# Down projection of the feed-forward stage: a different order of its weight units, and a split ahead of three additions to x

## The chip, the cores and the metric

The kernel runs on one core of one Trainium2 chip. The metric is the device time of one execution in microseconds (us); lower is better. Shown is the median of several runs, beside the time and the trace of one profiled execution.

## The reference, cut to what matters

Two blocks of two layers each work on x, 256 tokens by 1024 features in fp32. Every layer has two feed-forward stages (before and after a mixing stage), so there are eight of them:

```python
def swiglu(h, w1, w3, w2):
    return (jax.nn.silu(h @ w1) * (h @ w3)) @ w2

x = x + 0.5 * swiglu(rmsnorm(x, g), w1, w3, w2)      # w1, w3: 1024 x 2816, w2: 2816 x 1024
```

The change touches only the last product, with `w2`, called the down stage here.

## The kernel before, in words

**Splitting.** TensorE multiplies in fp32r. To keep fp32 accuracy every weight tile is split in two: ScalarE rounds it to `whi`, then VectorE computes the rest, `wlo = raw - whi`. Each product is three matmuls (hi by hi, hi by lo, lo by hi; lines 900, 902, 904 in `products`, lines 707, 708, 709 in `blocks`). The semaphores are `hi_done` (ScalarE's half is there), `w_ready` (VectorE's half too), `w_used` (TensorE is done with the unit). They are counters, so all engines go through the units in one common order.

**Units and buffers.** A unit is one slot of weights. Split units live in `split_w`, four slots (`HL`): ScalarE may split unit n only when TensorE is done with unit n - 4. Loads from HBM go to `raw`, three slots (`RAW`): the load of a unit may start only when VectorE has split the unit three loads earlier (SyncE waits in `load` on `w_ready`).

**The down stage.** 22 chunks of 128 hidden features are the depth. Ten of them are multiplied plainly: units ("plain", half, i), called P0, P1, P2 for the left 512 output columns and H0, H1, H2 for the right ones (here `half` 0 and 1). P0, P1, H0, H1 have 4 chunks (24 matmuls), P2 and H2 have 2 (12 matmuls). The other twelve are multiplied as 2 by 2 blocks with seven products instead of eight: U, 11, 21, T2, 22, T3, T4. Each of these has two units of 9 matmuls, a and b. The weights 11, 21, 22 are loaded to `raw`; U, T2, T3, T4 are sums of weight blocks. U, T2 and T4 are made in `early_sums` by accumulating DMAs that GpSimd issues (`down_sums`): T2 is U plus 22, T4 is T2 plus 21. T3 is made in `late_sums` by VectorE (`sum_added`), which adds the freshly loaded 22 to it. These sums take no slot of `raw`.

**The order.** The table `DOWN` gives the order of the units; ScalarE (`down_split` over the index), SyncE (`ffn_loads`) and the counts of all waits follow it. TensorE's and VectorE's code is written out in the same order by hand: in `ffn_tensor` behind `alone(0, 0, ...)`, in `ffn_vector` behind the loop over `i`. Before, it is

P0, Ua, Ub, 11a, 11b, 21a, 21b, P1, T2a, T2b, 22a, 22b, P2, T3a, T3b, T4a, T4b, H0, H1, H2.

VectorE also adds finished PSUM banks to x (`part_to_x`) between its splits. `used(i)` in front of one waits until TensorE is done with unit i, `split_before(i)` until VectorE's own split of unit i has ended. Banks: `EACH` is bank 0 (11, then T2, then T3 are accumulated there, with an addition to x taken between them; the semaphore `taken` tells TensorE that it may go on), `BOTH` is bank 1. Half way through H0, TensorE transposes the new x for the next stage; for that it waits until the last of these additions is done. `e.link` makes an engine wait for its own instruction.

Of the kernel before, what the change touches and what calls it, by code (L numbers as in the profile page):

```python
# [33 lines left out]
FG = FF // 256  # L34
# [8 lines left out]
SUPER, PAIRS = 2, 3  # L43
# [7 lines left out]
def each(kind, name):  # L51
    return tuple((kind, name, s) for s in range(SUPER))


DOWN = ((("plain", 0, 0),) + each("sum", "U") + each("quarter", "11") + each("quarter", "21") + (("plain", 0, 1),)
        + each("sum", "T2") + each("quarter", "22") + (("plain", 0, 2),) + each("sum", "T3") + each("sum", "T4")
        + tuple(("plain", 1, i) for i in range(3)))
# [149 lines left out]
def build(nc, a, known):  # L207
# [13 lines left out]
    with ctx:  # L221
# [460 lines left out]
        def _(eng):  # L682
# [112 lines left out]
            def ffn_tensor(u0, f, next_stage):  # L795
# [92 lines left out]
                def products(name):  # L888
# [3 lines left out]
                    for s in range(SUPER):  # L892
# [15 lines left out]
                def alone(half, i, start, stop):  # L908
                    blocks(u0 + 2 * FG + AT["plain", half, i], 0, 1 if half else 2, HT, ALONE[i], start, stop, True)
# [7 lines left out]
                products("21")  # L917
# [3 lines left out]
                products("T2")  # L921
                products("22")
                eng.wait_ge(ht_done, ffn_pairs(e, f, 10))
                alone(0, 2, False, (True, False))
                eng.wait_ge(taken, 2 * ffns(e, f) + 2)
# [915 lines left out]
        def _(eng):  # L1841
# [148 lines left out]
            def ffn_vector(u0, f, next_stage):  # L1990
# [117 lines left out]
                def splits(kind, name):  # L2108

                    for s in range(SUPER):  # L2110
                        i = at(kind, name, s)
                        added = [t for t, q in (("T2", "22"), ("T3", "22"), ("T4", "21")) if q == name and t in BY_VECTOR]
                        for t in added:
                            sum_added(u0 + 2 * FG + i, f, t, s)
                        down_split(i)

                splits("quarter", "11")
                splits("quarter", "21")
# [5 lines left out]
                splits("sum", "T2")  # L2124
                splits("quarter", "22")
                down_split(at("plain", 0, 2))
                used(at("sum", "T2"))
                split_before(at("plain", 0, 2))
                part_to_x(0, 1, EACH, minus_half).then_inc(taken, 1)
                splits("sum", "T3")  # L2130
                splits("sum", "T4")
                used(at("sum", "T3"))
                split_before(at("sum", "T4"))
                part_to_x(1, 0, EACH, rhalf)
                part_to_x(1, 1, EACH, minus_half)
                used(at("plain", 0, 2))
                part_to_x(0, 0, psum[:, 4, :], rhalf)
                down_split(at("plain", 1, 0))
                split_before(at("plain", 1, 0))
# [584 lines left out]
```

## Time and profile before

| what | value |
|---|---|
| median of 3 runs | 2255.55 us (2254.95 to 2256.36) |
| profiled execution, its time | 2255.33 us |
| profiled execution, its span | 2253.5 us |
| TensorE busy | 2226.4 us, 99% of the span |
| VectorE busy | 1711.6 us, 76% |
| ScalarE busy | 1305.8 us, 58% |
| DMA | 467.92 MB, mean 208 GB/s |
| granted TensorE clock | 1.0 of full speed on average |

Matmul records overlap (one starts every 0.23 us and is shown 0.39 us long), so idle time of TensorE is read best from the starts of its matmuls. A time such as t+8.16 below is counted from the first matmul of Ua in a stage. This matmul starts at 136.50 us in the first of the eight stages.

### The profile page before, as it was taken

The numbers are of one execution on the slowest core, as the hardware profiler recorded it, in microseconds if no ns is written. First come the engines' busy times: TensorE is split into PE (matmuls) and PEld (weight loads), VectorE is DVE, ScalarE is ACT, GpSimd is POOL, SyncE is SP. The second block draws the span as 40 slices with busy tenths as digits, with TensorE's granted clock in tenths as the row PEclk, the third lists the DMA queues.
The fourth block names the chain that finished last, engine by engine and source line by source line (L and its number), as shares of the span: only waits on it lengthen the run. The fifth ranks groups of instructions, "written<-read, shape, count | busy, mean of one in ns | idle before, by whom it ended". The sixth has DMA issues, their size and how long they took to land.

```text
span 2253.5 us, 28616 instructions
## 1 busy us (share of the span) xinstructions
PE 2226.4 (99%) x11542; PEld 1890.5 (84%) x11542; DVE 1711.6 (76%) x2067; ACT 1305.8 (58%) x1425; POOL 42.2 (2%) x52
## 2 busy tenths in 40 slices
PE   9999999999999999999999999999999999999999
PEld 8888888888887888887888888888888878888887
DVE  7876567868878566877887799768788777976876
ACT  7655445555655544655655676455565557754654
POOL 0000000000000000000000000000000000000000
PEclk9999999999999999999999999999999999999999
DMA  7876455767758455577576753547667575345756
GB/s 264 261 225 245 168 191 181 249 199 229 233 181 278 171 178 196 200 226 237 206 245 213 235 171 128 205 157 244 216 225 238 169 254 200 107 168 196 232 181 204
DMA packets 171859, 467.92 MB, mean 208 GB/s; under 512 B 18608, under 2 KB 22576, under 8 KB 171728
## 3 DMA queue, kind: packets, MB, share of 16 engines
q1 hardware_dynamic: 164672, 428.35, 53.8%
q0 software_dynamic: 6912, 37.75, 9.3%
q8 instruction: 91, 1.49, 0.3%
q14 instruction: 40, 0.33, 0.0%
q10 hardware_dynamic: 144, 0.00, 0.0%
HBM read 464.99 MB, written 1.05 MB: 207 GB/s over the span
## 4 chain that ended last, share of the span: by engine, by line
PE 87%; DVE 9%; DMA 2%; ACT 1%; issue 0%; SPq 0%; DVEq 0%; ACTq 0%
PE psum L771 25%; PE psum L772 13%; PE psum L707 12%; PE psum L709 12%; PE psum L708 12%; DVE split_w L1851 4%; PE psum L782 3%; PE psum L739 2%; PE psum L790 2%; DVE split_w L1858 1%; DVE x L2048 1%; DVE late_sums L1867 1%; PE psum L900 1%; PE psum L904 1%; PE psum L902 1%; DMA raw<-ffn_w_down_alone_dram 1%
## 5 line engine op out<-in xcount | busy, mean ns | idle before, releaser
L1851 DVE TENSOR_TENSOR split_w<-raw,split_w 128x2048 fp32r<-128x2048 f32 (+2 forms) x405 | 854.1, 2118 | 179.6 <-ACT split_w L1328 177.6
L771 PE MATMUL psum<-xt,split_w 128*128 128x512 f32 x2464 | 858.7, 393 | 0.5 <-DVE split_w L1851 0.5
L1328 ACT ACTIVATE split_w<-raw 128x2048 fp32r<-128x2048 f32 (+2 forms) x405 | 716.7, 1778 | 204.6 <-PE psum L709 95.2
L772 PE MATMUL psum<-xt,split_w 128*128 128x256 f32 x2464 | 688.1, 279 | 0.0
L771 PEld LDWEIGHTS psum<-xt,split_w 128*128 128x128 f32 x2464 | 461.3, 187 | 105.2 <-DVE split_w L1851 2.2
L772 PEld LDWEIGHTS psum<-xt,split_w 128*128 128x128 f32 x2464 | 464.9, 189 | 0.3
L707 PE MATMUL psum<-split_w,xt 128*128 128x512 f32 (+1 forms) x736 | 289.5, 393 | 0.0
L709 PE MATMUL psum<-split_w,xt 128*128 128x512 f32 (+1 forms) x736 | 283.7, 385 | 0.0
L708 PE MATMUL psum<-split_w,xt 128*128 128x512 f32 (+1 forms) x736 | 283.6, 385 | 0.0
L1997 DVE TENSOR_TENSOR gate_up<-psum,low 128x512 f32<-128x512 f32 x176 | 121.0, 688 | 144.1 <-ACT low L1403 144.1
L1403 ACT ACTIVATE low<-psum 128x512 f32<-128x512 f32 x176 | 104.1, 591 | 173.8 <-PE psum L772 158.3
L707 PEld LDWEIGHTS psum<-split_w,xt 128*128 128x128 f32 x736 | 138.3, 188 | 28.8 <-issue 3.0
L709 PEld LDWEIGHTS psum<-split_w,xt 128*128 128x128 f32 x736 | 138.2, 188 | 28.1
L708 PEld LDWEIGHTS psum<-split_w,xt 128*128 128x128 f32 x736 | 138.4, 188 | 25.6
L707 PE MATMUL psum<-split_w,ht_hi 128*128 128x512 f32 x316 | 125.3, 397 | 13.5 <-DVE split_w L1851 13.5
L1409 ACT ACTIVATE gate_up<-gate_up 128x512 f32<-128x512 f32 x88 | 55.7, 633 | 131.5 <-DVE gate_up L2004 131.5
L709 PE MATMUL psum<-split_w,ht_lo 128*128 128x512 f32 x316 | 123.3, 390 | 0.0
L708 PE MATMUL psum<-split_w,ht_hi 128*128 128x512 f32 x316 | 123.2, 390 | 0.0
L1349 ACT ACTIVATE xt<-psum,vecs 128x256 fp32r<-128x256 f32 x88 | 34.5, 476 | 108.1 <-PE psum L739 108.1
L782 PE MATMUL psum<-xt,split_w 128*128 128x512 f32 x352 | 86.1, 393 | 1.4 <-ACT split_w L1328 1.4
L2016 DVE TENSOR_TENSOR ht_lo<-hid,ht_hi 128x512 fp32r<-128x512 f32 x88 | 60.6, 688 | 35.3 <-ACT ht_hi L1414 35.3
L707 PEld LDWEIGHTS psum<-split_w,ht_hi 128*128 128x128 f32 x316 | 59.3, 188 | 31.8 <-issue 14.5
(305 smaller groups left out, 2839.2 us busy)
## 6 DMA issues: line engine op xcount, KB each, us to landing
raw<-w_in_dram SPq DMA_DIRECT2D x180, 512.0 KB, 4.4
raw<-t_gate_up_1b_dram SPq DMA_DIRECT2D x88, 512.0 KB, 4.7
raw<-t_gate_up_2a_dram SPq DMA_DIRECT2D x88, 512.0 KB, 4.7
raw<-t_gate_up_2b_dram SPq DMA_DIRECT2D x88, 512.0 KB, 4.7
raw<-t_gate_up_1a_dram SPq DMA_DIRECT2D x84, 512.0 KB, 4.8
early_sums<-ffn_w_down_quarters_dram POOLq DMA_DIRECT2D x24, 768.0 KB, 7.3
raw<-ffn_w_down_quarters_dram SPq DMA_DIRECT2D x48, 384.0 KB, 4.5
raw<-ffn_w_down_alone_dram SPq DMA_DIRECT2D x32, 512.0 KB, 7.1
```

The costliest lines, as they stand in the source:

```text
L707: nc.tensor.matmul(pair(p, m)[:, out], hi[:, c, t], whi[:, slot, w], start=first, stop=False)
L708: nc.tensor.matmul(pair(p, m)[:, out], hi[:, c, t], wlo[:, slot, w], start=False, stop=False)
L709: last = nc.tensor.matmul(pair(p, m)[:, out], lo[:, c, t], whi[:, slot, w], start=False, stop=final)
L771: nc.tensor.matmul(bank, whi[:, slot, w], xt[:, c, :, :], start=c == 0, stop=False)
L772: last = nc.tensor.matmul(bank[:, 0:T], wlo[:, slot, w], xt_hi[:, c, :], start=False, stop=c == DC - 1)
L782: nc.tensor.matmul(pair(p, j), whi[:, e.unit(u) % HL, first:first + P], xt[:, c, :, :], start=c == 0, stop=False)
L1328: nc.scalar.activation(whi[:, e.unit(u) % HL, 0:n], raw[:, r, 0:n], ACT.Copy).then_inc(hi_done, 1)
L1403: nc.scalar.activation(low[:, b % 2, :, :], psum[:, first:first + 2, T:2 * T], ACT.Copy).then_inc(low_done, 1)
L1409: nc.scalar.activation(gate_up[:, :, 0, :], gate_up[:, :, 0, :], ACT.Silu).then_inc(gate_done, 1)
L1851: nc.vector.tensor_tensor(wlo[:, e.unit(u) % HL, 0:n], raw[:, r, 0:n], whi[:, e.unit(u) % HL, 0:n], ALU.subtract).then_inc(w_ready, 1)
L1997: nc.vector.tensor_tensor(gate_up[:, b % 2, :, :], psum[:, first:first + 2, 0:T], low[:, b % 2, :, :], ALU.add).then_inc(pair_free, 1)
L2016: nc.vector.tensor_tensor(ht_lo[:, 2 * i:2 * i + 2, :], hid[:, :, :], ht_hi[:, 2 * i:2 * i + 2, :], ALU.subtract).then_inc(ht_done, 1)
```

## The change

`DOWN` becomes

P0, Ua, Ub, 11a, 11b, P1, T2a, 21a, T2b, 21b, P2, 22a, 22b, T3a, T3b, T4a, T4b, H0, H1, H2.

TensorE's and VectorE's code follow it. On VectorE the split of H0 now stands ahead of three additions to x (one from bank 4, two from bank 0), and the second addition of bank 0 is linked. The addition of T2 is now made before the sums for T3 and the splits of 22.

```diff
-DOWN = ((("plain", 0, 0),) + each("sum", "U") + each("quarter", "11") + each("quarter", "21") + (("plain", 0, 1),)
-        + each("sum", "T2") + each("quarter", "22") + (("plain", 0, 2),) + each("sum", "T3") + each("sum", "T4")
-        + tuple(("plain", 1, i) for i in range(3)))
+DOWN = ((("plain", 0, 0),) + each("sum", "U") + each("quarter", "11") + (("plain", 0, 1),)
+        + (("sum", "T2", 0), ("quarter", "21", 0), ("sum", "T2", 1), ("quarter", "21", 1), ("plain", 0, 2),) + each("quarter", "22")
+        + each("sum", "T3") + each("sum", "T4") + tuple(("plain", 1, i) for i in range(3)))
...
                 products("11")
-                products("21")
                 eng.wait_ge(ht_done, ffn_pairs(e, f, 9))
                 alone(0, 1, False, False)
                 eng.wait_ge(taken, 2 * ffns(e, f) + 1)
-                products("T2")
-                products("22")
+                for s in range(SUPER):
+                    products("T2", (s,))
+                    products("21", (s,))
                 eng.wait_ge(ht_done, ffn_pairs(e, f, 10))
                 alone(0, 2, False, (True, False))
+                products("22")
                 eng.wait_ge(taken, 2 * ffns(e, f) + 2)
...
-                splits("quarter", "11")
-                splits("quarter", "21")
+                for s in range(SUPER):
+                    down_split(at("quarter", "11", s))
                 down_split(at("plain", 0, 1))
                 used(at("quarter", "11"))
                 part_to_x(0, 0, EACH, rhalf).then_inc(taken, 1)
                 for m in range(MT):
                     part_to_x(m, 1, BOTH, rhalf)
-                splits("sum", "T2")
-                splits("quarter", "22")
+                for s in range(SUPER):
+                    down_split(at("sum", "T2", s))
+                    down_split(at("quarter", "21", s))
                 down_split(at("plain", 0, 2))
                 used(at("sum", "T2"))
-                split_before(at("plain", 0, 2))
+                split_before(at("sum", "T2"))
                 part_to_x(0, 1, EACH, minus_half).then_inc(taken, 1)
-                splits("sum", "T3")
-                splits("sum", "T4")
-                used(at("sum", "T3"))
-                split_before(at("sum", "T4"))
-                part_to_x(1, 0, EACH, rhalf)
-                part_to_x(1, 1, EACH, minus_half)
+                for s in range(SUPER):
+                    sum_added(u0 + 2 * FG + at("quarter", "22", s), f, "T3", s)
+                    down_split(at("quarter", "22", s))
+                for s in range(SUPER):
+                    down_split(at("sum", "T3", s))
+                for s in range(SUPER):
+                    down_split(at("sum", "T4", s))
+                down_split(at("plain", 1, 0))
                 used(at("plain", 0, 2))
                 part_to_x(0, 0, psum[:, 4, :], rhalf)
-                down_split(at("plain", 1, 0))
-                split_before(at("plain", 1, 0))
+                used(at("sum", "T3"))
+                part_to_x(1, 0, EACH, rhalf)
+                split_before(at("sum", "T4"))
+                e.link(part_to_x(1, 1, EACH, minus_half))
                 used(at("sum", "T4"))
```

What it moves on the engines, first on VectorE: the down stage of the first feed-forward, from the splits of the loaded 11 units (the first row holds 11 and 21) to the split of P2 and the addition of T2. `split_w<-raw` are splits of loaded units (1536 elements a row: 11, 21, 22; 2048: P1; 1024: P2), `split_w<-early_sums` those of T2, `late_sums<-late_sums,raw` the sums for T3, `x<-psum` additions to x. Before:

```order
L1851 TENSOR_TENSOR split_w<-raw,split_w 128x1536 [waits hi_done] x4
L1851 TENSOR_TENSOR split_w<-raw,split_w 128x2048 [waits hi_done]
L2048 SCALAR_TENSOR_TENSOR x<-psum,rhalf,x 128x512 [waits w_used]
L2048 SCALAR_TENSOR_TENSOR x<-psum,rhalf,x 128x512 x2
L1858 TENSOR_TENSOR split_w<-early_sums,split_w 128x1536 [waits hi_done] x2
L1867 TENSOR_TENSOR late_sums<-late_sums,raw 128x1536 [waits late_in0,raw_in1]
L1851 TENSOR_TENSOR split_w<-raw,split_w 128x1536 [waits hi_done]
L1867 TENSOR_TENSOR late_sums<-late_sums,raw 128x1536 [waits late_in1,raw_in2]
L1851 TENSOR_TENSOR split_w<-raw,split_w 128x1536 [waits hi_done]
L1851 TENSOR_TENSOR split_w<-raw,split_w 128x1024 [waits hi_done]
L2048 SCALAR_TENSOR_TENSOR x<-psum,minus_half,x 128x512 [waits w_ready,w_used]
```

VectorE with the change, from the split of P1 to the sum of T3b:

```order
L1852 TENSOR_TENSOR split_w<-raw,split_w 128x2048 [waits hi_done]
L2049 SCALAR_TENSOR_TENSOR x<-psum,rhalf,x 128x512 [waits w_used]
L2049 SCALAR_TENSOR_TENSOR x<-psum,rhalf,x 128x512 x2
L1859 TENSOR_TENSOR split_w<-early_sums,split_w 128x1536 [waits hi_done]
L1852 TENSOR_TENSOR split_w<-raw,split_w 128x1536 [waits hi_done]
L1859 TENSOR_TENSOR split_w<-early_sums,split_w 128x1536 [waits hi_done]
L1852 TENSOR_TENSOR split_w<-raw,split_w 128x1536 [waits hi_done]
L1852 TENSOR_TENSOR split_w<-raw,split_w 128x1024 [waits hi_done]
L2049 SCALAR_TENSOR_TENSOR x<-psum,minus_half,x 128x512 [waits w_ready,w_used]
L1868 TENSOR_TENSOR late_sums<-late_sums,raw 128x1536 [waits late_in0,raw_in2]
L1852 TENSOR_TENSOR split_w<-raw,split_w 128x1536 [waits hi_done]
L1868 TENSOR_TENSOR late_sums<-late_sums,raw 128x1536 [waits late_in1,raw_in0]
```

The two splits of 21 have moved from ahead of P1 to between those of T2, and the addition of T2, which waits for TensorE (`w_used`), has moved from behind the splits of 22 to ahead of the sums for T3.

On VectorE behind that, around the split of H0 (2048). Before:

```order
L2048 SCALAR_TENSOR_TENSOR x<-psum,rhalf,x 128x512 [waits w_ready,w_used]
L2048 SCALAR_TENSOR_TENSOR x<-psum,minus_half,x 128x512
L2048 SCALAR_TENSOR_TENSOR x<-psum,rhalf,x 128x512 [waits w_used]
L1851 TENSOR_TENSOR split_w<-raw,split_w 128x2048 [waits hi_done]
L2048 SCALAR_TENSOR_TENSOR x<-psum,rhalf,x 128x512 [waits w_used,w_ready]
```

With the change:

```order
L1852 TENSOR_TENSOR split_w<-raw,split_w 128x2048 [waits hi_done]
L2049 SCALAR_TENSOR_TENSOR x<-psum,rhalf,x 128x512 [waits w_used] x2
L2049 SCALAR_TENSOR_TENSOR x<-psum,minus_half,x 128x512 [waits w_ready]
L2049 SCALAR_TENSOR_TENSOR x<-psum,rhalf,x 128x512 [waits w_used,dve_own]
```

The split of H0 stands first, and the last addition waits for VectorE's own one before it (`dve_own`).

On SyncE the loads of the same stage (each unit is two DMAs; 128x1024 twice is P1, 128x768 are 11, 21, 22 and the two `late_sums`, 128x512 twice is P2):

```order
 L502 DMA raw<-w_a_alone_dram 128x1024 x2
-L502 DMA raw<-w_a_quarters_dram 128x768 x8
+L502 DMA raw<-w_a_quarters_dram 128x768 x4
 L502 DMA raw<-w_a_alone_dram 128x1024 x2
+L502 DMA raw<-w_a_quarters_dram 128x768 x4
+L502 DMA raw<-w_a_alone_dram 128x512 x2
 L537 DMA late_sums<-w_a_quarters_dram 128x768 x4
 L502 DMA raw<-w_a_quarters_dram 128x768 x4
-L502 DMA raw<-w_a_alone_dram 128x512 x2
```

The load of P1 moves ahead of those of 21, and the load of P2 ahead of `late_sums` and 22.

## Rows read from the trace of the kernel before

**Rows 1.** Page, part 1: busy time, share of the span, count of instructions

```profile
PE 2226.4 (99%) x11542; PEld 1890.5 (84%) x11542; DVE 1711.6 (76%) x2067; ACT 1305.8 (58%) x1425; POOL 42.2 (2%) x52
```

**Rows 2.** TensorE's waits: line, releaser, us in total, times, longest

```profile
PE psum L707 <- DVE split_w L1851: 13.5, 16, 1.7
PE psum L900 <- DVE split_w L1851: 6.8, 8, 2.0
...
PE psum L771 <- DVE split_w L1851: 0.5, 1, 0.5
```

**Rows 3.** Windows, first matmul of Ua to that of H0: us, PE busy, clock, DMA

```profile
136.50:176.69 40.19, 37.80 (x163) 1.00 0.93 299
...
1797.77:1839.16 41.39, 37.79 (x163) 1.00 0.81 254
...
sum 323.01, PE 302.21; mean PE 37.78
```

**Rows 4.** Timeline of TensorE, first stage; Ua, 21b, P1, T2a, 22a, 22b, H0

```profile
136.50 0.39 PE L900 MATMUL psum<-split_w,sa_hi 128*128 128x512 f32 x1
...
147.67 0.50 PE L900 MATMUL psum<-split_w,ht_hi 128*128 128x512 f32 x1 [0.81 <-DVE split_w L1851]
...
151.27 0.47 PE L707 MATMUL psum<-split_w,ht_hi 128*128 128x512 f32 x1 [1.26 <-DVE split_w L1851]
...
156.83 0.39 PE L900 MATMUL psum<-split_w,sa_hi 128*128 128x512 f32 x1
...
160.91 0.39 PE L900 MATMUL psum<-split_w,sa_hi 128*128 128x512 f32 x1
...
163.16 0.50 PE L900 MATMUL psum<-split_w,sa_hi 128*128 128x512 f32 x1
...
176.69 0.50 PE L707 MATMUL psum<-split_w,ht_hi 128*128 128x512 f32 x1 [0.28 <-DVE split_w L1851]
```

**Rows 5.** Timeline of ScalarE, first stage; splits of 21a, 21b, 22a

```profile
138.80 1.49 ACT L1328 ACTIVATE split_w<-raw 128x1536 fp32r<-128x1536 f32 x1 [0.55 <-PE psum L904]
144.33 1.49 ACT L1328 ACTIVATE split_w<-raw 128x1536 fp32r<-128x1536 f32 x1 [4.04 <-DMA raw<-w_a_quarters_dram]
...
153.02 1.49 ACT L1328 ACTIVATE split_w<-raw 128x1536 fp32r<-128x1536 f32 x1 [1.48 <-DMA raw<-w_a_quarters_dram]
```

**Rows 6.** Timeline of VectorE, first stage: start, us, instruction, count

```profile
136.86 5.22 DVE L1851 TENSOR_TENSOR split_w<-raw,split_w 128x1536 fp32r<-128x1536 f32 x3
...
148.83 2.29 DVE L1851 TENSOR_TENSOR split_w<-raw,split_w 128x2048 fp32r<-128x2048 f32 x1 [1.22 <-ACT split_w L1328]
151.04 2.06 DVE L2048 SCALAR_TENSOR_TENSOR x<-psum,rhalf,x 128x512 f32<-128x512 f32 x3
153.01 3.42 DVE L1858 TENSOR_TENSOR split_w<-early_sums,split_w 128x1536 fp32r<-128x1536 f32 x2
156.35 1.75 DVE L1867 TENSOR_TENSOR late_sums<-late_sums,raw 128x1536 f32<-128x1536 f32 x1
...
161.36 2.89 DVE L1851 TENSOR_TENSOR split_w<-raw,split_w 128x1536 fp32r<-128x1536 f32 x2
...
172.38 0.75 DVE L2048 SCALAR_TENSOR_TENSOR x<-psum,rhalf,x 128x512 f32<-128x512 f32 x1 [0.61 <-PE psum L904]
...
174.36 2.28 DVE L1851 TENSOR_TENSOR split_w<-raw,split_w 128x2048 fp32r<-128x2048 f32 x1
```

**Rows 7.** Timeline of SyncE, first stage: start, us until the last one's end, DMAs

```profile
113.25 26.25 SPq L502 DMA_DIRECT2D raw<-w_a_quarters_dram  x8
...
143.34 5.11 SPq L502 DMA_DIRECT2D raw<-w_a_quarters_dram  x4
```

**Rows 8.** Timeline of ScalarE, seventh stage; split of 21b

```profile
1806.83 1.49 ACT L1328 ACTIVATE split_w<-raw 128x1536 fp32r<-128x1536 f32 x1 [5.26 <-DMA raw<-ffn_w_down_quarters_dram]
```

**Rows 9.** The first stage's window: all engines busy, clock, DMA share, GB/s

```profile
142.00:154.00 12.00, 9.94 (x43) 7.60 (x42) 7.01 (x7) 7.13 (x5) 0.00 (x0) 1.00 1.03 406
```

**Rows 10.** Accumulating DMAs of the first stage, from issue to landing

```profile
DMA to landing us min/median/max: 6.7/7.1/10.3
```

More of the change, by code:

```diff
@@ L886, in ffn_tensor, with products @@
                        "22": (pair(1, 0), True, False)}
-                def products(name):
+                def products(name, groups=range(SUPER)):
                     out, start, stop = OUT[name]
                     resumed = name in ("T2", "T3")
-                    for s in range(SUPER):
+                    for s in groups:
                         u = u0 + 2 * FG + AT["quarter" if name in QUARTERS else "sum", name, s]
@@ L2106, in used @@
                     multiplied(u0 + 2 * FG + i)
[L2108 to L2115, printed above, removed]
-                splits("quarter", "11")
-                splits("quarter", "21")
+                for s in range(SUPER):
+                    down_split(at("quarter", "11", s))
                 down_split(at("plain", 0, 1))
```

## The prediction, written before the changed kernel ran

> **What bounds the kernel now.** The page first: TensorE is busy for 2226.4 of 2253.5 us [rows 1], so only its gaps can be won. The list of TensorE's waits names them: 24 waits of 20.3 us in all on VectorE's splits, 8 of them in front of line 900 (6.8 us) and 16 in front of line 707 (13.5 us) [rows 2]; there is almost nothing else. Both lines are code of the down stage, and eight stages make it three waits each: ahead of 21b, of P1 and of H0 [rows 4].
>
> The windows of the eight stages, from the first matmul of Ua to the first of H0, hold 323.01 us, 40.38 each, 40.19 in the first and 41.39 in the seventh [rows 3]. What would they be without a gap? In the first stage the 18 matmuls of T2a and T2b start at 156.83 and 22a at 160.91 [rows 4]: 4.08 us, 0.2267 each, so a unit of 9 takes 2.04, one of 12 takes 2.72, one of 24 takes 5.44. A window has 162 matmuls: 36.73 us. So **3.65 us are lost in a stage, 29.2 in all**; 20.3 of that are waits [rows 2], and the rest is slower matmuls behind each wait (0.50 instead of 0.39 in the rows) and a small gap ahead of 22b. The granted clock is 1.00 in these windows [rows 3].
>
> **Why the splits are late.** In times counted from t = 136.50: TensorE starts 21b at t+11.17, where gapless it would be t+10.20, and P1 at t+14.77 [rows 4]. ScalarE had split 21a from t+2.30 on and then waited 4.04 us for 21b's load, to t+7.83 [rows 5]. That load may start only when VectorE has split 11a; SyncE's eight DMAs of 11 and 21 end at t+3.0 [rows 7], so 21b's first was issued near t+2.1, as one unit takes about 0.9 to issue. From issue to landing: 5.7 us, and 6.9 in the seventh stage (t0 = 1797.77 there, ScalarE starts at 1806.83) [rows 3, 8]. P1 is one load further behind, and its split takes 2.29 us of VectorE, begun at 148.83 [rows 6], so TensorE waits again. Four loaded units of 2.04 us each follow one another, against three slots of `raw`; the loads can't keep that pace.
>
> **The change, part by part.**
>
> *P1 ahead of T2 and 21.* Its load takes the place that 21a's had, issued at 113.25 [rows 7], so it has long landed. ScalarE can split it from t+2.30 [rows 5], in the slot that Ua leaves; 1.9 us later, at about t+4.2, VectorE follows, which is through with 11b by 0.36 + 1.67 + 1.75 = t+3.8 (start of its three splits [rows 6], 1.67 from one to the next by the pair 153.01 to 156.35 [rows 6]). P1 is ready at t+6.5 and wanted at t+8.16. **The wait ahead of P1 goes.**
>
> *T2 and 21 alternating.* 11b ends at t+8.16, its `w_used` comes 0.2 later; then three additions (1.97 us from 151.04 to 153.01 [rows 6]) to t+10.3, and the splits of T2a, 21a, T2b at 1.67 apiece: ready at t+12.1, 13.7 and 15.4. TensorE, in P1 until t+13.60, wants them at 13.60, 15.64, 17.68. 21a's load is now the one issued at t+2.1, landed by t+7.8 to 9.1, and nobody is waiting for it. 21b needs P1's slot of `split_w`: ScalarE from t+13.8 to 15.3, VectorE to t+17.1; wanted at 19.72. P2: VectorE to t+18.2, wanted at 21.76. **The wait ahead of 21b goes**, with 2 us to spare.
>
> *The addition of T2.* It now stands ahead of the sums for T3, and waits until T2b has been multiplied, which 21a pushes back to t+19.72, plus 0.2 until the record ends and the addition starts (as 172.38 does behind T3b [rows 6]). VectorE is idle from 18.2 to 19.93: this is the **new wait**. Queued behind it are, in this order: 0.66 for the addition, sum for T3a to t+22.26, split of 22a to t+24.0, sum for T3b to 25.6, split of 22b to t+27.36 (1.67 a step, the last one 1.75 long). 22a is wanted at t+24.48: in time. 22b is wanted at t+26.52: TensorE waits about 0.9 us with the 0.05 that it needs to start (163.11 against 163.16 in the first stage [rows 4, 6]). In the kernel before, the same unit already starts 0.2 late, from the same chain of sums and splits. I add 0.15 for slower matmuls behind the wait, as its 22b shows. From below this cost can't go under 0 and from above it is set by the loads, next.
>
> *Loads of 22.* 22a's slot is free when 21a is split, t+13.7; it must have landed by t+20.6, in 6.9 us. 22b: from t+17.1 to t+23.9, 6.8 us. The nearest rows: 21b's 5.7 us, and 6.9 in the seventh stage [rows 5, 8], taken while the accumulating DMA for T2b ran, as that for T4a will here. The far row: 22a in the kernel before, issued at 143.34, landed at 153.02, 9.7 us [rows 5, 7]. But at that time P1, `late_sums` and 22 stood in the queues together, at 406 GB/s with the DMA engines full [rows 9]. With the change P1 is gone from that heap and 22 is issued 7 us later, when `late_sums` (1.5 MB, issued from about t+7) is through. I take 5.7 to 6.9: hidden, barely. The Trainium skill, DMA: Bandwidth & Descriptors, section Anatomy of one DMA, fits 2.0 us plus the bytes at 436 GB/s for DMAs issued by GpSimd: for the 768 KB of a unit an estimate of 3.8 us. No row here is as short for a unit's two DMAs; by the page the sum stays as it is, by the 9.7 us row (22a at t+23.4, 2.8 late, 1.05 + 2.8 = 3.85 lost in a stage) it would come to 2257.
>
> *H0's split ahead of three additions.* VectorE goes on from 22b at t+27.3 with T3a, T3b, T4a, T4b to t+34.0 and H0 (2.28) to t+36.2. ScalarE's half of H0 needs T3a's slot, free at t+31.8. H0 is wanted at t+37.8 with the new wait in it: **the wait of 0.28 and its slow start go**, 0.44 us. What was ahead of it comes later: the additions run from t+36.2, the last one behind T4b (t+38.0) ends near t+39.1, its link included. TensorE wants it for the transposes after 12 matmuls of H0, t+40.5. Hidden; without that cover, it costs what it is late, some 0.1 us for the link. H1's split follows at t+39.1 to 41.3 and is wanted at 44.3.
>
> **The sum.** Lost in a stage with the change: 0.9 + 0.15 = 1.05 us, 8.4 in all. Gain 29.2 - 8.4 = 20.8 us. The profiled execution took 2255.33, 1.8 more than its span, which the change leaves alone, and 0.2 less than the median of 2255.55: 2255.55 - 20.8 = 2234.75, **2235 us**.
>
> **Rivals.**
> 1. *No new wait* (chance 0.08). If T2b ends sooner for VectorE than I count or the splits catch up, 22b is in time: 29.2 - 8 x 0.2 = 27.6 won, 2228. Against it: the chain behind the addition has no slack in my count.
> 2. *22 lands late, about a microsecond past its time* (0.10). Then every later split moves with it: 8 x 1 us less, 2243. For it: only 0 to 1.2 us of slack, and the DMA engines are much used in these windows (299 GB/s in the first [rows 3]).
> 3. *The gain is given back behind the stage* (0.05). Next stages' splits would have to be late by the 2.5 us won; TensorE has no such wait there today but for 0.5 us at line 771 [rows 2]. 2255.
> 4. *Slower* (0.05). Mechanism: 22's load in a full queue. A stage breaks even when 22a lands 2.6 us late (3.65 - 1.05), 9.5 us after issue. Accumulating DMAs, which now share the queues with it, have taken up to 10.3 us [rows 10]: at that, 22a lands at t+24.0, 3.4 us late, the stage loses 1.05 + 3.4 = 4.45 instead of 3.65, eight of them +6.4: 2262. Against it: the heap of rows 9 is pulled apart by the change.
>
> That the order isn't changed as said is excluded by the rows of the program's order.
>
> **How the numbers follow.** Forecast as worked out, 2235: 0.72. Its own spread is 0.5 us a stage in when the new wait starts and ends, 4 us in all, 2231 to 2239. The range takes in part of rivals 1 and 2: 2229 to 2243, which leaves out half of rival 1, rivals 3 and 4 and some of 2. This kernel's runs tell a difference of 0.2%, 4.5 us, from none. Faster than that: forecast, rivals 1 and 2, 0.90. Within: 0.06, slower: 0.04 (rival 4 for the most part, 3 for the first).
>
> **What would show it.** In the trace of the changed kernel: no wait of TensorE at line 707 in front of P1 and H0; at line 901, where line 900 now stands, eight waits, in front of 22b and not of 21b, near 0.9 us each; VectorE idle for about 1.7 us on TensorE ahead of the addition with `minus_half`; ScalarE's wait for the loads of 21 and 22 without effect on TensorE; windows of the eight stages near 36.73 + 1.05 = 37.8 us. I am wrong if TensorE waits in front of 22a or T3 (late loads), in front of T2a (three additions too slow), or in stages behind, where it does not now.

## The result, and the profile after

| | before | after |
|---|---|---|
| median | 2255.55 us (2254.95 to 2256.36) | 2278.71 us (2274.15 to 2283.07) |
| profiled execution | 2255.33 us | 2281.0 us |
| its span | 2253.5 us | 2279.2 us |
| TensorE busy | 2226.4 us | 2236.2 us |
| granted TensorE clock, mean | 1.000 | 0.990 |

The ratio of after to before is 1.0102, with a 95% interval of 1.008 to 1.0125. The change costs 23 us; 2235 us had been forecast, 20.8 less than before.

Two rows of the profile already say that two things went wrong, not one. The first fence is part 1 of the page of the changed kernel, which answers to [rows 1]. The second is its list of TensorE's waits (line, releaser, us in total, times, longest), which answers to [rows 2].

```profile
PE 2236.2 (98%) x11542; PEld 1903.0 (83%) x11542; DVE 1711.8 (75%) x2067; ACT 1305.3 (57%) x1425; POOL 42.1 (2%) x52
```

```profile
PE psum L900 <- DVE split_w L1852: 36.5, 10, 5.9
...
PE psum L771 <- DVE split_w L1852: 0.6, 1, 0.6
```

All waits at line 707, those for P1 and H0, are gone, as forecast. But at line 900 there are 36.5 us in ten waits of up to 5.9 us, where the prediction had eight of some 0.9 us (it put them at line 901, but that matmul still stands at line 900). Eight of the ten are ahead of 22a, one in each stage, 1.43 to 5.94 us; the other two, 2.61 and 0.42, are ahead of 22b in the third and the fifth stage. And TensorE is *busy* for 9.8 us more with the same 11542 matmuls: some of them ran slowly.

The windows of the stages, from the first matmul of Ua to that of H0, answer to [rows 3]. This is TensorE's view: us, PE busy (count), clock, DMA share, GB/s. The first, the fifth and the last stage are shown.

```profile
136.73:180.91 44.18, 38.77 (x164) 0.92 0.88 267
...
1232.46:1273.72 41.26, 38.92 (x163) 0.96 0.89 271
...
2217.54:2262.22 44.68, 39.49 (x164) 0.92 0.77 229
```

A stage without a gap takes 36.73 us. These lose 7.45, 4.53 and 7.95; the eight together lose 7.45, 8.85, 6.26, 8.36, 4.53, 7.32, 5.14 and 7.95, in all 55.9 us. Before they lost 29.2. The difference, 26.7, covers the growth of the span, 25.7. So the whole loss is in the down stages.

**Where in a stage.** TensorE's timeline of the first stage (t = 136.73) shows one wait, ahead of 22a:

```profile
160.98 0.39 PE L709 MATMUL psum<-split_w,ht_lo 128*128 128x512 f32 x1
166.78 0.79 PE L900 MATMUL psum<-split_w,sa_hi 128*128 128x512 f32 x1 [5.41 <-DVE split_w L1852]
...
170.66 0.40 PE L900 MATMUL psum<-split_w,sa_hi 128*128 128x512 f32 x1
```

P2's last matmul starts at 160.98, then nothing until 166.78, which is t+30.05 where t+24.48 was forecast. The chain that ended last, here in the piece from the split of 21a to 22a's first matmuls (start, us, what), says who was waited for:

```profile
148.82 1.68 DVE split_w L1852
...
150.51 0.33 SPq L502
...
150.89 12.39 DMA raw<-w_a_quarters_dram
...
163.30 1.55 DVE late_sums L1868
...
164.97 1.76 DVE split_w L1852
...
166.78 0.79 PE psum L900
167.57 0.43 PE psum L902
...
170.82 0.23 PE psum L900
```

VectorE ends the split of 21a, SyncE issues the load of 22a at 150.51 (t+13.8, to a tenth where the prediction put it), and that load lands 12.8 us later, at 163.30. Over the eight stages the load of 22a takes 8.8 to 13.3 us (mean 11.5), and that of 22b 10.2 to 11.7. Behind 22a's stand the sum for T3a and the split, 3.5 us (the prediction had left 3.9 for them). Up to 170.6 the matmuls behind the wait start 0.43 us apart, then 0.23 again. ScalarE, waiting for the same load, shows it too (answers to [rows 5]):

```profile
163.30 1.48 ACT L1329 ACTIVATE split_w<-raw 128x1536 fp32r<-128x1536 f32 x1 [9.61 <-DMA raw<-w_a_quarters_dram]
```

**What else was in the queues.** SyncE's timeline (answers to [rows 7]) and GpSimd's, both of the first stage:

```profile
144.14 2.10 SPq L537 DMA_DIRECT2D late_sums<-w_a_quarters_dram  x4
150.51 4.23 SPq L502 DMA_DIRECT2D raw<-w_a_quarters_dram  x4
```

```profile
149.36 0.87 POOL L1818 DMA_DIRECT2D early_sums<-w_a_quarters_dram  x1 [12.67 <-DVE split_w L1859]
152.77 0.86 POOL L1818 DMA_DIRECT2D early_sums<-w_a_quarters_dram  x1 [2.54 <-DVE split_w L1859]
```

And GpSimd's timeline of the kernel before, the same two instructions:

```profile
155.30 0.88 POOL L1817 DMA_DIRECT2D early_sums<-w_a_quarters_dram  x1 [18.85 <-DVE split_w L1858]
157.05 0.86 POOL L1817 DMA_DIRECT2D early_sums<-w_a_quarters_dram  x1 [0.87 <-DVE split_w L1858]
```

These are the accumulating DMAs that turn T2 into T4. GpSimd may issue one when VectorE has split the same half of T2 (`early_sums` is free then). Before, that was t+18.8 and t+20.5, and 22a had landed at t+16.5 [rows 5]. The change splits T2 some 6 us sooner, so they go out at t+12.6 and t+16.0: just ahead of 22a's load, and in the middle of 22's four DMAs. Nobody needs T4 at that time; where no load is late, TensorE reaches T4a at t+33.6 (second experiment). The window from 149.00 to 163.30 (all engines' busy time, clock, DMA share, GB/s) beside the window of before from 128.00 to 140.00, in which T2's accumulating DMAs are nearly alone:

```profile
149.00:163.30 14.30, 12.37 (x55) 9.92 (x53) 6.76 (x6) 2.56 (x3) 1.74 (x2) 1.00 1.02 281
```

```profile
128.00:140.00 12.00, 12.00 (x62) 10.26 (x61) 8.06 (x8) 5.93 (x6) 1.76 (x2) 1.00 0.61 107
```

The DMA engines are full, but at 281 GB/s, not at the 406 of [rows 9]. The other window tells why: there two accumulating DMAs hold the engines for 0.61 of the time and move only 107 GB/s. Per byte that is 0.61/107 against 1.03/406, 2.2 times as much.

**The clock.** Windows of all engines over the wait, the unit behind it, and the next one:

```profile
161.20:166.78 5.58, 0.17 (x1) 0.00 (x1) 3.48 (x3) 3.10 (x3) 0.00 (x0) 0.72 0.88 326
166.78:170.66 3.88, 3.88 (x10) 3.06 (x10) 3.88 (x3) 2.73 (x2) 0.00 (x0) 0.52 0.71 227
170.66:172.75 2.09, 2.09 (x11) 1.69 (x10) 2.09 (x2) 1.49 (x1) 0.00 (x0) 1.00 0.94 318
```

After 5.4 us without work the nine matmuls of 22a ran at a granted clock of 0.52, the lower level (1.2 GHz), and took 3.88 us instead of 2.04. This late load so cost about 1.8 us more than its wait. The clock fell once in each of the eight stages; of the 55.9 us that the stages lose, 36.5 are the waits, and the other 19.4, 2.4 in a stage, are slow matmuls.

### The profile page after: what moved, and what is told of

It reads as the page before. It is cut to its first block, busy times and chain, and to the rows that moved or that the text cites. A ratio compares the mean times of both kernels' runs of the same rounds, so it can differ in the third digit from the quotient of the medians.

```text
span 2279.2 us, 28608 instructions
## 1 busy us (share of the span) xinstructions
PE 2236.2 (98%) x11542; PEld 1903.0 (83%) x11542; DVE 1711.8 (75%) x2067; ACT 1305.3 (57%) x1425; POOL 42.1 (2%) x52
## 4 chain that ended last, share of the span: by engine, by line
PE 90%; DMA 5%; DVE 4%; ACT 0%; SPq 0%; issue 0%; DVEq 0%; ACTq 0%
PE psum L771 25%; PE psum L772 13%; PE psum L707 12%; PE psum L709 12%; PE psum L708 12%; PE psum L782 3%; PE psum L900 3%; PE psum L902 2%; PE psum L904 2%; DMA raw<-ffn_w_down_quarters_dram 2%; DVE split_w L1852 2%; PE psum L739 2%; PE psum L790 2%; DMA raw<-w_b_quarters_dram 1%; DMA raw<-w_a_quarters_dram 1%; DVE x L2049 1%
## 5 line engine op out<-in xcount | busy, mean ns | idle before, releaser
L900 PE MATMUL psum<-split_w,sa_hi 128*128 128x512 f32 x192 | 83.0, 432 | 36.5 <-DVE split_w L1852 36.5
```

What stands on the lines that cost most here:

```text
L900: nc.tensor.matmul(out, hi, whi[:, slot, w], start=start and s == 0 and k == 0, stop=False, skip_group_check=resumed)
```

## The experiments

The theory after this reading: **T4's accumulating DMAs, issued 4 to 6 us sooner, make 22's load late, and everything else of the change does what was forecast.** Rivals: it is the bytes in the queue and not the adding; it is the other order of loads (P1 ahead, P2 and `late_sums` beside 22) whatever GpSimd does; or the new wait ahead of the addition costs more than counted.

### T4's DMAs behind 22's loads

```diff
+                            if name == "T4":
+                                late = u0 + 2 * FG + AT["quarter", "22", s]
+                                eng.wait_ge(raw_in[e.place(late) % RAW], loaded(e, late))
                             accumulate(ADDED[name], s, w2)
```

> The changed kernel, but GpSimd issues the accumulating DMAs of T4a and T4b only when the loads of 22a and 22b have landed. Theory A (the accumulating DMAs of T4, which the change issues at t+12.7 and t+16.1, hold up the loads of 22, issued from t+13.8): 22a lands within 7 us of its issue, TensorE no longer waits ahead of 22a and about 0.9 us ahead of 22b, the clock stays at full speed, windows of the eight stages near 37.8 us, 2235 us in all. T4a's own sum, issued near t+20, lands near t+28 and is in time. Theory B (the loads of 22 are slow by themselves, since they are issued late and follow late_sums): 22a still lands near t+26, and the time stays near 2275 us.

2264.69 us (2262.74 to 2267.27), ratio to before 1.0038 [1.0025, 1.0052]. TensorE's waits:

```profile
PE psum L900 <- DVE split_w L1862: 18.0, 8, 2.8
PE psum L900 <- DVE split_w L1855: 5.7, 8, 0.7
```

The second row is the eight waits ahead of 22b, 0.71 each: 22a is in time in every stage. So the accumulating DMAs were what made it late. The first row is new: T4b is late now. GpSimd's and ScalarE's timelines of the first stage (t = 137.21) give issue and landing:

```profile
155.62 0.88 POOL L1818 DMA_DIRECT2D early_sums<-w_a_quarters_dram  x1 [18.45 <-DVE split_w L1855]
159.14 0.86 POOL L1818 DMA_DIRECT2D early_sums<-w_a_quarters_dram  x1 [2.65 <-DMA raw<-w_a_quarters_dram]
```

```profile
166.25 1.49 ACT L1338 ACTIVATE split_w<-early_sums 128x1536 fp32r<-128x1536 f32 x1 [1.84 <-DMA early_sums<-w_a_quarters_dram]
171.28 1.49 ACT L1338 ACTIVATE split_w<-early_sums 128x1536 fp32r<-128x1536 f32 x1 [3.54 <-DMA early_sums<-w_a_quarters_dram]
```

They take 10.6 and 12.1 us (9.9 to 13.3 over the eight stages) beside the loads that follow, H0's among them. Expected were some 8 us and 2235 us in all. The DMAs can't simply be moved: sooner they hold up 22, later they are late themselves.

### T4's DMAs made small, and T4 copied instead of added

In the first, T4's DMAs add 16 of 1536 columns:

```diff
-                            accumulate(ADDED[name], s, w2)
+                            if name == "T4":
+                                eng.dma_start(early_sums[:, s, 0:16], quarter(e, w2, ADDED[name], s)[:, 0:16],
+                                              accum_op=ALU.add).then_inc(added_in[s], 16)
+                            else:
+                                accumulate(ADDED[name], s, w2)
```

> The changed kernel, but the accumulating DMAs of T4 move 16 of 1536 columns, at the same points of the program. This leaves nearly all of the bytes of T4's sum out of the computation. Theory A: 22a lands within 6 us of its issue, windows near 37.8 us, about 2235 us. Theory B: near 2275 us. If this one is fast and the run with T4 behind 22 is not, the point of issue was not enough.

In the second they move all the bytes, from GpSimd as before, but don't add:

```diff
+                            if name == "T4":
+                                eng.dma_start(early_sums[:, s, :], quarter(e, w2, ADDED[name], s)).then_inc(added_in[s], 16)
```

> The changed kernel, but the DMAs of T4 copy the same 768 KB each, from the same queue, without adding; the sum of T4 is left out of the computation. Under theory A this tells bytes from the adding. If an accumulating DMA is dear only for its bytes, the time stays near 2278 us. If the adding is what is dear (in the kernel before, the DMA engines' share was 0.61 at only 107 GB/s while two of them ran, against 1.03 at 406 GB/s for plain loads), 22a lands some 4 us sooner than in the changed kernel and the time falls to 2240 to 2250 us. Theory B: no change, 2275 us.

The small one took **2233.41 us** (2233.12 to 2235.89), ratio 0.9901 [0.9888, 0.9915]; the copy 2241.72 (2238.2 to 2245.87), ratio 0.9942 [0.9927, 0.9957]. The first is the forecast of 2235 to within 2 us. Its waits, and then those of the copy:

```profile
PE psum L900 <- DVE split_w L1856: 5.7, 8, 0.7
```

```profile
PE psum L900 <- DVE split_w L1855: 9.9, 9, 1.6
```

ScalarE's timeline of the first stage shows 22a's landing, first of the small one, whose load was issued at 152.48, then of the copy, issued at 150.50:

```profile
157.84 1.49 ACT L1329 ACTIVATE split_w<-raw 128x1536 fp32r<-128x1536 f32 x1 [2.19 <-DMA raw<-w_a_quarters_dram]
```

```profile
156.79 1.49 ACT L1329 ACTIVATE split_w<-raw 128x1536 fp32r<-128x1536 f32 x1 [3.12 <-DMA raw<-w_a_quarters_dram]
```

5.4 us and 6.3 us, against 12.8 with the accumulate; over the eight stages 4.2 to 5.6, and 6.2 to 6.7 with one of 8.9. The copy's nine waits are eight ahead of 22b and, in the fourth stage, one ahead of 22a. So the bytes of T4 at that place cost 8 us of the whole time, and the adding another 37 (2278.7 less 2241.7). The order of the other loads is no cause: both kernels have it unchanged. What adding takes from the DMA engines is read from part 3 of the page (GpSimd's queue: packets, MB, share of 16 engines over the span), of the changed kernel, the small one and the copy:

```profile
q0 software_dynamic: 6912, 37.75, 9.2%
```

```profile
q0 software_dynamic: 6912, 25.30, 6.7%
```

```profile
q0 software_dynamic: 6912, 37.75, 7.9%
```

In microseconds of all sixteen engines: 9.2% of 2279.2 is 209.7, 6.7% of 2234.1 is 149.7, 7.9% of 2236.4 is 176.7. Against the small one, the sixteen DMAs for T4 hence take 60 us when they add and 27 when they copy, 3.8 and 1.7 us each. The small ones take something too: the kernel with T4 by VectorE, below, has no such DMA, and its queue 6.4% of 2241.7, 143.5 us. Against that it is 4.1 and 2.1 us each. Either way, adding costs about twice a copy of the same bytes.

### The other parts of the change

H0's split ahead of three additions, put alone into the kernel before:

```diff
-                used(at("sum", "T3"))
-                split_before(at("sum", "T4"))
-                part_to_x(1, 0, EACH, rhalf)
-                part_to_x(1, 1, EACH, minus_half)
+                down_split(at("plain", 1, 0))
                 used(at("plain", 0, 2))
                 part_to_x(0, 0, psum[:, 4, :], rhalf)
-                down_split(at("plain", 1, 0))
-                split_before(at("plain", 1, 0))
+                used(at("sum", "T3"))
+                part_to_x(1, 0, EACH, rhalf)
+                split_before(at("sum", "T4"))
+                e.link(part_to_x(1, 1, EACH, minus_half))
```

> The kernel before with the second part of the change alone: H0's split ahead of three additions to x. By the prediction's step the wait of 0.28 us ahead of H0 and its slow start go in each of eight stages, 0.44 us each: 3.5 us less, 2252 us. The rival: the additions, now later, delay the transposes in H0 or H1's split, and the time stays at 2255.5 us.

2252.35 us against 2256.64 of the kernel before beside it, ratio 0.9983 [0.9975, 0.9992]: 4.3 us won (1.8 to 5.6 by the interval), 3.5 forecast. No stage waits ahead of H0 any more; the eight windows of the profiled execution lose 26.7 us instead of 29.2.

The other disputed cost is the new wait of VectorE ahead of the addition of T2. It goes when the addition stands behind the splits of 22. With T4's DMAs small, so that loads can't blur it:

```diff
-                used(at("sum", "T2"))
-                split_before(at("sum", "T2"))
-                part_to_x(0, 1, EACH, minus_half).then_inc(taken, 1)
                 for s in range(SUPER):
                     sum_added(u0 + 2 * FG + at("quarter", "22", s), f, "T3", s)
                     down_split(at("quarter", "22", s))
+                used(at("sum", "T2"))
+                split_before(at("sum", "T2"))
+                part_to_x(0, 1, EACH, minus_half).then_inc(taken, 1)
```

> The kernel with the small T4 (16 of 1536 columns, nearly all of T4's sum left out), and the addition of T2 behind the splits of 22. By the prediction's step the wait of 0.71 us ahead of 22b and what follows it, 1.0 us in a stage, come from VectorE's wait on T2b alone: without it the windows of the eight stages are 36.7 us and the time is 2233.4 - 8 = 2225.5 us. The rival, that VectorE simply has too much work there: the wait stays, at least in part.

2225.78 us (2224.76 to 2226.52), ratio 0.9863 [0.9849, 0.9878], 7.6 less than with the addition early. The window of its first stage, all engines:

```profile
136.79:173.51 36.72, 36.72 (x163) 30.41 (x162) 33.99 (x25) 24.05 (x16) 1.74 (x2) 1.00 0.86 279
```

This is the gapless 36.73 on which the prediction's losses were measured, now seen in a trace: nothing is lost. The new wait cost 1.0 us a stage, as counted.

### Other times for T4's DMAs

Three runs looked for a time at which both T4 and 22 are in time. Only T4b behind 22b's load (the first diff with `if name == "T4" and s == 1`):

> The changed kernel; the accumulating DMA of T4a stays where the change puts it (t+12.7), only that of T4b waits until 22b has landed. If the delay of 22's loads comes from the bytes in work at once, one of the two sums should delay 22a by about half of what both did: 22a starts 1 to 3 us late instead of 1.4 to 5.9, and T4b, issued near t+24 and alone, lands in some 8 us, in time for t+34. About 2255 us, between the changed kernel's 2278 and the 2233 of the small T4. If T4a alone is what holds up 22a, the wait ahead of 22a stays near 5 us and the time at 2270.

2250.0 us (2247.63 to 2251.4), ratio 0.9971 [0.9959, 0.9982]. T4a's DMA still runs beside 22's loads: TensorE waits eight times ahead of 22a, 9.0 us in all and up to 2.4 at once, and six times ahead of 22b, some 1.0 each. T4b's DMA, issued at t+23.9 to 26.2, lands in 7.2 to 9.8 us and is late in one stage alone. The same with the addition late:

> The kernel of the run with T4b behind 22b, and VectorE's addition of T2 moved from ahead of the sums for T3 to behind the splits of 22. Where 22a lands in time, this takes away the wait of 0.9 us ahead of 22b; where it lands late, nothing. Between 0 and 8 us less than that run.

2253.11 us (2250 to 2256), ratio 0.9984 [0.9975, 0.9994]: nothing won, and 3 us more than in that run, which the expectation did not allow for. Where the load is late, the wait of VectorE that the edit removes is hidden behind it, and 22b waits 1.0 us all the same: its split ends a sum and a split, 3.34 us, behind that of 22a, and TensorE is through with 22a sooner. And both DMAs behind 22a's load, the addition late (`late` with "22", 0 for both halves):

> The changed kernel with both accumulating DMAs of T4 behind the landing of 22a, and the addition of T2 behind the splits of 22. In the run with both behind 22's own loads the wait ahead of T4b was 2.0 to 2.8 us, since its sum was issued at t+21.9 and took 12.1 us. Here it is issued 2.6 us sooner, so that wait should be 0 to 1 us, and that ahead of 22b is gone: about 2235 to 2245 us. If the sum for T4b takes longer the sooner it is issued (it then runs beside that of T4a and the load of 22b), the wait ahead of T4b stays near 2 us and the time near 2256.

2272.02 us (2265.9 to 2274.07), ratio 1.0064 [1.0047, 1.008]. This is 27 us beyond the upper end of what was expected, and 16 beyond the time named for a slow T4b. Its waits:

```profile
PE psum L900 <- DVE split_w L1862: 29.2, 16, 3.9
```

All sixteen T4 units are late. T4a's DMA, issued at t+18.8, lands at t+30.5, 11.7 us later; T4b, whose DMA is released at the same time, at t+35.6. Issued sooner than in the first experiment, T4b landed 1.5 us *later*: the two accumulating DMAs now ran beside each other, 22b, H0 and the rest.

### T4 made by an engine

T4 is T2 plus 21, and 21 lies in `raw` anyway. VectorE can add it there and no DMA is needed:

```diff
-BY_VECTOR = ('T3',)
+BY_VECTOR = ('T4', 'T3')
...
                     down_split(at("sum", "T2", s))
+                    sum_added(u0 + 2 * FG + at("quarter", "21", s), f, "T4", s)
                     down_split(at("quarter", "21", s))
```

with the addition of T2 late as above.

> The changed kernel without any accumulating DMA for T4: VectorE makes T4a and T4b from the raw 21 that is loaded anyway, ahead of its splits of 21 (two more additions of 1.67 us in each stage), and the addition of T2 stands behind the splits of 22. By the theory that those DMAs are what delays 22, 22a's load lands within 6 us of its issue and no wait on a load is left. VectorE becomes the bound: by its rows 21b is ready at t+20.45 against 19.72 wanted, 22b at t+28.3 against 27.45, T3a 0.2 late; 2.2 us lost in a stage with the slow matmuls behind the waits instead of 3.65, about 2244 us. If the loads of 22 are slow for another reason, 22a's wait stays at 1.4 us and more, and the time stays above 2260.

2243.82 us (2243.11 to 2244.18), ratio 0.9944 [0.9928, 0.9961], as expected to 0.2 us. In the first stage 22a's load takes 4.25 us from issue (151.31) to landing (155.56). What is left is 16 waits of 10.4 us, on VectorE, which does 2 x 1.67 us more per stage behind an addition that starts late.

The same by GpSimd, whose engine is idle, 22's loads waiting for its sums:

```diff
+                for s in range(SUPER):
+                    part = u0 + 2 * FG + AT["quarter", "21", s]
+                    r = e.place(part) % RAW
+                    eng.wait_ge(w_ready, units(e, u0 + 2 * FG + AT["sum", "T2", s], RAW))
+                    eng.wait_ge(raw_in[r], loaded(e, part))
+                    nc.gpsimd.tensor_tensor(early_sums[:, s, :], early_sums[:, s, :], raw[:, r, 0:QUARTER],
+                                            ALU.add).then_inc(pool_sum, 1)
```

> As the run with T4 by VectorE, but GpSimd, idle for 98% of the span, makes the two sums; 22a and 22b are loaded when the sums that read the raw 21 are done. No row shows such an addition on GpSimd. If it takes up to 2.5 us, 22a (issued from t+14.5) and 22b (t+17.9) are in time and the windows near 36.8 us: about 2227 us. At 5 us each, 22b's load is issued at t+22, it lands at t+27.5, and TensorE waits 4 us for it in each stage: 2257 us. The two engines may also slow each other: then VectorE's splits of 21 and T2b, beside it, take more than 1.75 us.

2269.96 us (2269.85 to 2270.05), ratio 1.006 [1.0045, 1.0075], 13 us above the higher of the two times expected. GpSimd's and then VectorE's timeline of the first stage:

```profile
148.20 4.96 POOL L1842 TENSOR_TENSOR early_sums<-early_sums,raw 128x1536 f32<-128x1536 f32 x1 [12.22 <-DVE split_w L1871]
```

```profile
148.02 1.75 DVE L1864 TENSOR_TENSOR split_w<-raw,split_w 128x1536 fp32r<-128x1536 f32 x1
149.69 5.08 DVE L1871 TENSOR_TENSOR split_w<-early_sums,split_w 128x1536 fp32r<-128x1536 f32 x1
```

GpSimd's sum is recorded with 4.96 us. The split of VectorE that was already running when it began keeps its 1.75; the next one takes 5.08 instead: it ends 1.6 us, one split, after GpSimd's sum (153.16). From the end of the first split (149.77) to the end of the sum, 3.4 us, VectorE seems to stand still. If GpSimd in turn stood still during the first split, its work alone is 3.4 us and not 4.96; all sixteen sums overlap splits in this way, so no run shows one alone. Nothing is offloaded: 3.3 us of VectorE are spent to save it 1.67. The Trainium skill, SBUF — State Buffer, section Who interferes with whom, has the rule: an instruction of VectorE with both inputs in SBUF contends with one of GpSimd that reads SBUF, and the later one is blocked. This trace agrees.

Half and half, T4a by VectorE and T4b by a DMA behind 22b's load:

> Between two earlier runs: T4a by VectorE from the raw 21a, T4b by an accumulating DMA that waits until 22b has landed; addition of T2 behind the splits of 22. VectorE has one sum of 1.67 us less than with both: 21b is in time (t+18.8 for 19.72), 22b comes out within 0.2 us of its time. T4b's DMA, alone of its kind and issued near t+23.5, lands after 8 to 12 us, at t+31.5 to 35.5, wanted at about t+31.5: a wait ahead of T4b of 0 to 4 us. Theory: 1 to 3 us lost in a stage, 2235 to 2250 us; if the one accumulating DMA is as slow as in the run with both behind 22 (12.1 us), 2258.

2259.26 us (2253.68 to 2261.51), ratio 1.0007 [0.9997, 1.0016]. T4b waits eight times, 19.5 us, as in the first experiment: its DMA, issued at t+23.4 to 23.7, lands after 10.4 to 12.0 us. That a single one is too much at that time does not follow: in the run with only T4b behind 22b's load it was issued a little later and landed in 7.2 to 9.8. There the loads behind it in time were issued some 1 us after it; here two go out together with it (at t+23.3 and 23.6, beside 23.5). Whether that is what makes the difference was not tried.

Last, T4 by VectorE with two of the three additions for which VectorE stood idle (1.82 us in the row at 145.09 below) taken ahead: those of bank 1, which need only U.

```diff
-                used(at("quarter", "11"))
-                part_to_x(0, 0, EACH, rhalf).then_inc(taken, 1)
+                used(at("sum", "U"))
                 for m in range(MT):
                     part_to_x(m, 1, BOTH, rhalf)
+                used(at("quarter", "11"))
+                part_to_x(0, 0, EACH, rhalf).then_inc(taken, 1)
```

> The run with T4 by VectorE, and the two additions of bank 1 to x (which need U alone) ahead of the wait for 11b, in the 1.8 us in which VectorE is idle there. Its chain then runs 1.3 us sooner: 21b is ready at t+19.1 (19.72 wanted), 22b at t+26.95 (26.52 wanted), so one wait of 0.45 us is left in a stage where there were 0.7 twice, and T3a's 0.3. Lost: 0.6 us in a stage, 5 in all, against 29.2 in the kernel before: about 2232 us. If VectorE's work as such were not what bounds that run, it stays at 2244.

**2233.45 us** (2232.67 to 2233.91), ratio 0.9896 [0.9881, 0.991]: faster than both kernels, with the whole computation in it. Part 1 of its page and its longest group of waits:

```profile
PE 2221.4 (100%) x11542; PEld 1891.8 (85%) x11542; DVE 1735.2 (78%) x2083; ACT 1303.8 (58%) x1425; POOL 28.2 (1%) x36
```

```profile
PE psum L900 <- DVE split_w L1852: 2.7, 8, 0.4
```

A stage loses 0.9 to 1.1 us here, and 2232 had been expected. This is the changed order with its gain, once T4's DMAs are out of the way and three of VectorE's additions to x are moved as well.

## Why the prediction was wrong, point by point

- **What bounds the kernel; why the splits were late.** Right. With T4's DMAs made small and the addition of T2 late the stage takes the gapless 36.72 us, and nothing outside the stages appeared.
- **P1 ahead of T2 and 21; T2 and 21 alternating.** Right, to a tenth or two. VectorE's timeline of the changed kernel (answers to [rows 6]):

```profile
145.09 2.07 DVE L2049 SCALAR_TENSOR_TENSOR x<-psum,rhalf,x 128x512 f32<-128x512 f32 x3 [1.82 <-PE psum L904]
147.07 1.75 DVE L1859 TENSOR_TENSOR split_w<-early_sums,split_w 128x1536 fp32r<-128x1536 f32 x1
...
156.65 0.75 DVE L2049 SCALAR_TENSOR_TENSOR x<-psum,minus_half,x 128x512 f32<-128x512 f32 x1 [1.64 <-PE psum L904]
```

  T2a is split from t+10.3 (10.3 forecast). TensorE waits nowhere ahead of P1, T2, 21 or P2.
- **The addition of T2.** Right: it starts at t+19.92, behind 1.64 us of idleness (forecast 19.93 and 1.7). Its price ahead of 22b, 0.9 and 0.15, is 0.88 and 0.13 to 0.16 in the kernel with T4's DMAs small, and 7.6 us of the whole against the 8.4 counted.
- **Loads of 22.** This step failed. It read "I take 5.7 to 6.9: hidden, barely"; it was 12.8 in the first stage. Over the eight stages it was 8.8 to 13.3, and the load of 22b, for which 6.8 were left, took 10.2 to 11.7. The term rested on the row of 21b in the kernel before, with one accumulating DMA beside it, and on the belief that the heap of [rows 9] is pulled apart. It was not: `late_sums`, taken to be through by then, landed at t+15.0 to 17.2, after 22a's load was issued at t+13.8. That alone would have been hidden, as the kernel with T4's DMAs small shows, where 22a takes 5.4 us beside it. The prediction had noted that T4a's DMA would run there, without working out when the change lets GpSimd issue both: behind T2's splits, which moved from t+16.5 to t+10.3 and from t+18.2 to t+13.7. Two units of accumulating DMA, 3.8 us of all engines each, came into a gap of 6.9 us that already held the end of `late_sums` and 22's own 1.5 MB. The far row, 9.7 us, was nearer, and even it was too short: the cost has no bound in a row in which the same DMAs stood elsewhere.
- **The Trainium skill's estimate.** DMA: Bandwidth & Descriptors, section Anatomy of one DMA, gave an estimate of 3.8 us for a unit. Where no accumulating DMA of a whole unit runs beside it, 22a takes 4.25 us (T4 by VectorE) and 5.4 (T4's DMAs small) in the first stage; in the changed kernel 12.8. Here the estimate was a floor, and no forecast for a full queue. The same page of the Trainium skill, in Rules for kernel authors, says that an accumulate reads its destination and writes it later. That would fit the double price, 3.8 against 1.7 us, but no run here separates the read from the add.
- **H0's split ahead.** Right: 4.3 us measured alone, 3.5 forecast. In the first stage H1 starts 6.33 us behind H0 after the change and 6.51 before, where its matmuls alone take 5.44; the transposes between them, which wait for the last addition, so take no longer than before.
- **The clock.** Missing from the sum. The prediction's price for a late unit was its wait and 0.15. Against the kernel with T4's DMAs small the changed one has 30.8 us more of waits at line 900 (36.5 less 5.7) and 15.6 us more of TensorE's busy time (2236.2 less 2220.6). Together that is 46.4, and the medians are 45.3 apart. So a third of the loss against that kernel was slow matmuls. By the clock's records in the two traces TensorE was busy for 35.1 us at the lower level in the changed kernel and for 3.2 in the other; half of the difference is 16.0 us, which is all of it. None of the prediction's cases had that in it.
- **The rivals.** The fourth named the mechanism, 22's load in a full queue with accumulating DMAs beside it, and the point from which it decides, 9.5 us from issue to landing. It was given 0.05. Its own price, 2262, was 17 us short: it had 10.3 us for the landing (on average 11.5), nothing for a late 22b, and no clock. The break-even at 9.5 us does not hold for the same reasons: in the third and the fifth stage 22a landed after 8.8 and 9.3 us, and they lost 6.26 and 4.53 us, more than the 3.65 of before. The second, a microsecond late, is what a plain copy would have done.

## What to carry to other kernels

When a step moves to an earlier place, list every DMA that waits for it, on all queues, work out its new issue time, and lay it over the transfers that are wanted next: a transfer that nobody needs yet can push out the one that everybody needs. Price an accumulating DMA by the share of the DMA engines that its queue shows in the profile, not by its bytes, and where its second operand is on chip anyway, let an engine with slack add it. Where a forecast has a wait of two microseconds or more on TensorE, look in the trace at what the clock did behind such waits, and charge it.

## What the runs showed of the hardware

- **Adding in a DMA costs about twice a copy.** 768 KB took 3.8 us of all sixteen DMA engines added and 1.7 copied (4.1 and 2.1 against a kernel without such a DMA). T4's sums landed 9.9 to 13.3 us after issue in the first experiment. The load of 22a, 768 KB too, took 4.1 to 4.3 us without such DMAs (T4 by VectorE), 6.2 to 6.7 and once 8.9 beside copies of the same bytes, and 8.8 to 13.3 beside two that add.
- **The clock fell behind some waits and not behind others.** Behind 5.4 us it was 0.52 for 3.88 us. In the fifth stage of the changed kernel it fell behind only 1.92 us, and in the seventh of the kernel before it did not behind 2.02, although TensorE had been multiplying without a gap before both. The rows (TensorE's view) are the stretch behind the wait after the change, and then, with the wait in it, the unit of the kernel before:

```profile
1259.02:1261.50 2.48, 2.48 (x7) 0.56 1.03 422
```

```profile
1807.97:1812.00 4.03, 2.00 (x9) 1.00 1.04 410
```

  In the kernel before with H0's split ahead, the same seventh stage had a wait of 1.94 us in the same place, and there the clock did fall, 1.2 us behind it (0.66 on average over the unit). What decides between the two was not tried.
- **GpSimd and VectorE held each other up on tensor_tensor.** Beside a sum of GpSimd that is recorded with 4.96 us, a split of VectorE took 5.08 us instead of 1.75, 3.3 more.
